# Two more gate blocks ahead of the first projection products in the merge of a hybrid attention and recurrence layer

## The reference, cut to what matters

```python
h = rms_norm(x, norm_g) * (1 + scale) + shift
qa, ka, va, za, qb, fb, ib, zb = split(h @ w_in)
ya = window_attention(qa, ka, va, sinks) * silu(za)        # width 512
o, s_new = hgrn2_chunked(qb, log_f(fb), k_in(fb), ib, s0)   # width 512
yb = rms_norm(o, o_norm_g) * silu(zb)
g_a, g_b = split(sigmoid(h @ w_merge + b_merge))            # 1024 each
y = g_a * (ya @ w_proj_a) + g_b * (yb @ w_proj_b)
out = x + gate * (y @ w_out)
```

## Time and profile before

| | |
|---|---|
| three runs, median | 1559.14 us (1557.93 to 1559.82) |
| span of the profiled execution | 1555.9 us |
| PE busy | 1527.1 us (98%) |
| DVE, ACT, POOL busy | 787.0, 540.7, 826.0 us |
| mean granted TensorE clock | 0.996 |

### The profile page before, as it was taken

How to read it: one execution, slowest core, us unless ns; L and a number is a source line. 1 busy time by engine, 2 the same in 40 slices (tenths; PEclk the granted TensorE clock), 3 DMA queues, 4 the chain that set the end, 5 groups by cost and what they waited for, 6 DMA issues and landing times.

```text
span 1555.9 us, 31655 instructions
## 1 busy us (share of the span) xinstructions
PE 1527.1 (98%) x13048; PEld 1243.0 (80%) x13048; DVE 787.0 (51%) x1900; ACT 540.7 (35%) x1119; POOL 826.0 (53%) x1074
## 2 busy tenths in 40 slices
PE   5999999999999999999999999999999999999998
PEld 2777788877888788888779878888888978888886
DVE  4767464234558866232544774622453775623132
ACT  4334324334322532434331452243432353143330
POOL 0525434557863643365773472437786363437671
PEclk9999999999999999999999999999999999999999
DMA  9612211334453321233343231223544231222351
GB/s 339 243 55 83 83 57 55 111 133 158 168 197 108 110 70 57 82 109 108 137 164 135 92 120 43 83 66 114 208 154 149 75 110 56 78 72 91 102 167 60
DMA packets 62790, 178.94 MB, mean 115 GB/s; under 512 B 7086, under 2 KB 18695, under 8 KB 61864
## 3 DMA queue, kind: packets, MB, share of 16 engines
q1 hardware_dynamic: 62648, 176.93, 33.4%
HBM read 162.84 MB, written 11.96 MB: 112 GB/s over the span
## 4 chain that ended last, share of the span: by engine, by line
PE 95%; DVE 3%; DMA 1%; SPq 1%; issue 1%; ACT 0%; DVEq 0%
PE ps_D L758 56%; PE ps_D L755 25%; PE ps_XCD L820 2%; PE ps_XB L896 1%; PE ps_XB L949 1%; PE ps_XA L954 1%; PE ps_XA L921 1%; PE ps_XA L932 1%; PE ps_XB L948 1%; PE ps_XA L896 1%; DMA th_t<-in_w_ada 1%; SPq L507 1%; PE ps_XB L932 0%; PE ps_XCD L831 0%; PE ps_XCD L939 0%
## 5 line engine op out<-in xcount | busy, mean ns | idle before, releaser
L1702 POOL TENSOR_TENSOR w_lo_t<-w_raw,w_hi_t 128x256 fp32r<-128x256 f32 x920 | 681.0, 775 | 599.7 <-ACT w_hi_t L980 599.4
L758 PE MATMUL ps_D<-h_hi_t,w_hi_t 128*128 128x512 f32 x1024 | 411.2, 402 | 0.0
L758 PE MATMUL ps_D<-h_hi_t,w_lo_t 128*128 128x512 f32 x1024 | 399.6, 390 | 0.0
L758 PE MATMUL ps_D<-h_lo_t,w_hi_t 128*128 128x512 f32 x1024 | 399.5, 390 | 0.0
L980 ACT ACTIVATE w_hi_t<-w_raw 128x1024 fp32r<-128x1024 f32 x232 | 240.0, 1051 | 124.6 <-PE ps_D L755 61.6
L758 PEld LDWEIGHTS ps_D<-h_hi_t,w_hi_t 128*128 128x128 f32 x1024 | 192.3, 188 | 46.3 <-issue 8.9
L758 PEld LDWEIGHTS ps_D<-h_hi_t,w_lo_t 128*128 128x128 f32 x1024 | 192.2, 188 | 41.8
L758 PEld LDWEIGHTS ps_D<-h_lo_t,w_hi_t 128*128 128x128 f32 x1024 | 192.6, 188 | 36.5
L755 PE MATMUL ps_D<-w_hi_t,h_hi_t 128*128 128x384 f32 (+1 forms) x384 | 141.6, 369 | 1.0 <-DVE yf_t L1342 1.0
L755 PE MATMUL ps_D<-w_lo_t,h_hi_t 128*128 128x384 f32 (+1 forms) x384 | 136.6, 356 | 0.0
L755 PE MATMUL ps_D<-w_hi_t,h_lo_t 128*128 128x384 f32 (+1 forms) x384 | 136.3, 355 | 0.0
(11 more groups left out here) (386 smaller groups left out, 2332.9 us busy)
## 6 DMA issues: line engine op xcount, KB each, us to landing
w_raw<-in_w_blocks SPq DMA_DIRECT2D x232, 512.0 KB, 3.4
xr<-in_x_prompt SPq DMA_DIRECT2D x16, 512.0 KB, 5.0
x_or_AT<-in_x_prompt SPq DMA_DIRECT2D x14, 512.0 KB, 4.8
out_dram<-xr SPq DMA_DIRECT2D x12, 512.0 KB, 2.8
x_or_AT<-in_x_turned SPq DMA_DIRECT2D x3, 1024.0 KB, 5.6
p_or_hf<-in_x_turned SPq DMA_DIRECT2D x3, 1024.0 KB, 6.2
out_dram<-xr SPq DMA_DIRECT2D x8, 256.0 KB, 2.0
ibtok<-vtok SPq DMA_DIRECT2D x8, 192.0 KB, 3.5
```

The source lines that it names most:

```text
L758: ins = mm(bank[:, :], w[:, s0, k0 + k, :], a[:, k, :], start=go, stop=end)
L1702: ins = g_.tensor_tensor(w_lo[:, c, k:k + 2], w_raw[:, n % NRAW, k:k + 2], f32(w_hi[:, c, k:k + 2]), ALU.subtract)
```

## The change

The order of the units from 36 on becomes

| units | before | after |
|---|---|---|
| 36, 37 | pa0 pb0 | ga4 gb4 |
| 38 to 41 | pa1 pb1 pa2 pb2 | pa0 pb0 pa1 pb1 |
| 42, 43 | ga4 gb4 | pa2 pb2 |
| 44, 45 | pa3 pb3 | ga5 gb5 |
| 46, 47 | ga5 gb5 | pa3 pb3 |
| 48, 49 | pa4 pb4 | ga6 gb6 |
| 50, 51 | ga6 gb6 | pa4 pb4 |
| 52 to 59 | pa5 pb5 ga7 gb7 pa6 pb6 pa7 pb7 | the same |

The weight blocks follow that order. `ga4` and `gb4` get two new places, 8 and 9, in `ff`, and ACT waits for `st 3` before it writes them. `ga5`, `ga6` and `ga7` (with their `gb`) move to places 0, 2 and 0. The tasks `xst 2` and `xst 3` move from 40.1 and 41.1 to 42.1 and 43.1. SP's event `x01` moves from 43 to 44, its event `ckv 0` from 40 to 41, and the first group of the sample attention from 43 to 44.

```diff
-    out = [(c, j) for j in range(4) for c in ("ga", "gb")]
+    out = [(c, j) for j in range(5) for c in ("ga", "gb")]
     for j in range(8):
-        out += [("pa", j), ("pb", j)] + ([("ga", j + 2), ("gb", j + 2)] if 1 < j < 6 else [])
+        out += [("pa", j), ("pb", j)] + [(c, {2: 5, 3: 6, 5: 7}[j]) for c in ("ga", "gb") if j in (2, 3, 5)]
...
-            put(it, (40, 41, 46, 47)[_n], 1, "xst", _t)
+            put(it, (42, 43, 46, 47)[_n], 1, "xst", _t)
...
-            _u = (43, 52)[_r]
+            _u = (44, 52)[_r]
...
-TH.update({(c, j): (4, 6, 0, 2, 0, 2, 0, 2)[j] + (c == "gb") for j in range(8) for c in ("ga", "gb")})
+TH.update({(c, j): (4, 6, 0, 2, 8, 0, 2, 0)[j] + (c == "gb") for j in range(8) for c in ("ga", "gb")})
...
             n = TH[(kind, j)]
+            if n >= 8:
+                return ff[:, n - 8, :]
             return th[:, n, :] if n < 4 else (R2, R3)[n // 2 - 2][:, TB * (n % 2):TB * (n % 2) + TB]
...
-                    later.setdefault(b0 + 43, []).append(("x01", it, 0))
+                    later.setdefault(b0 + 44, []).append(("x01", it, 0))
...
-            later.setdefault(40, []).append(("ckv", 0, 0))
+            later.setdefault(41, []).append(("ckv", 0, 0))
...
                     if (kind, j) == ("ga", 0):
                         s.freed(it, "PV", 3)
+                    if (kind, j) == ("ga", 4):
+                        s.freed(it, "st", 3)
```

## The result

The changed kernel takes 1561.09 us (median of 12 runs, 1559.36 to 1562.31) against 1557.45 us of the kernel before (12 runs, 1556.02 to 1559.82; its median was 1559.14 in the three runs known ahead). The ratio is 1.0021, with a 95% interval of 1.0012 to 1.0029: slower by 3.3 us. The forecast was slower by 5.0 us, and 1564 us as a time.

A forecast was written before the change was run, and what follows sets the result against it. PE's stream was taken to bound the kernel. The terms -0.2 + 1.7 + 1.5 + 2.0 = +5.0 us on the span of 1555.9 gave 1560.9, with 3.2 us around it 1564.1, forecast as 1564; range 1558.5 to 1571.5.

The forecast's parts named there:

- What bounds the kernel, and what the order can win: PE's stream bounds the kernel; PE doesn't wait for `yb_lo` at pb0, so more units in between win nothing.
- The loss through `rstd`: DVE's chain now stands between the fetches of pa4 and pb4; PE waits 1.7, 1.5 and 2.0 us in iterations 0 to 2.
- The two paces of the chain: DVE's 17 `rstd` operations take 0.20 us each with POOL idle, 0.70 with POOL working: 3.4 to 11.9 us.
- the column sum ahead of `sT 1`: Iteration 0: DVE's column sum, which empties bank XC, stands behind the chain, so PE waits 1.7 us at `sT 1`.
- The covered wait for bank D1: Iteration 2: pb5 needs D1, freed by pb4's fetch at 1126.3; `bc` keeps PE busy to 1126.4, so no added wait.
- the sum's negative side: Iteration 1 on PE: pa4 and pa5 become neighbours, two `bu` become one pair; -0.2 us, ends 0 and -0.6.
- the term for the time around the span: 3.2 us added around the forecast span of 1560.9 us to give the time of 1564.1 us.
- (a): Rival, chance 0.20: POOL idle when `rstd` starts, the chain takes 3.4 us and is hidden; not slower, 1559 us.
- (b): Rival, chance 0.12: the chain stays 7.8, 6.3 and 10.3 us long; waits together 12.3 us, time 1571 us.
- (c): Rival, chance 0.07: the cache rows come late in iteration 0, +2.4 us, 1566.5 us.
- (d): Rival, chance 0.06: each of three PE waits is followed by 3 us at half clock, 1.5 us more each, 1568.5 us.
- (e): Rival, chance 0.05: faster, PE's 1.5 and 0.7 us waits vanish; with the `bu` pair 2.4 us, 1557 us.

The follow-up runs named there:

- experiment 2: Changed kernel with PE's `bc` one unit later (53.1 instead of 52.1), `rstd` left in place; 1562.83 us, ratio 1.0032 to the kernel before.
- experiment 6: Kernel before with the sample attention's two groups a unit later (44 and 53 instead of 43 and 52); 1557.11 us, ratio 0.9996.
- experiment 4: Changed kernel with the split of block `pa6` on ACT and POOL moved from unit 50 to 52 in iterations 0 to 2; 1562.12 us.
- experiment 3: Changed kernel with 12 more operations in the `rstd` chain, 29 instead of 17, in iterations 0 to 2; 1574.43 us.

## Why the prediction was right and wrong

**What bounds the kernel, and what the order can win.** Right. PE's stream sets the end, and pa0 and pb0 are fetched without a wait in both orders. Iteration 3, which has the new order and nothing else, is unchanged to 0.01 us.

**The loss through `rstd`.** Right in mechanism and place, and near in size. The prediction had 1.7, 1.5 and 2.0 us for the three iterations, 5.2 together. Taking the chain out of the sandwich gave back 1.65, 1.51 and 1.84, together 5.0. The two paces of the chain, POOL's schedule that sets their mix and the column sum ahead of `sT 1` came as worked out. In iteration 2 the chain was to end at 1125.6 and `bc` to be due at 1123.65, with the second kernel's start as before; the profile has 1124.7 and 1123.27, an earlier start of the iteration and a slightly shorter wait. The covered wait for bank D1 is there as well: experiment 2 uncovered it.

**The step that failed** is the sum's negative side, and beside it the term for the time around the span. The prediction said that "the matmuls, splits and weight blocks are the same in number" and that one side effect saves PE work, "I take -0.2". The pair came (L814 of 128x128 falls from 64 to 32 instructions in iteration 1) and was worth -0.41. Larger is what was left out: the sample tasks of iteration 0 move too, and their own queue for bank XC was not gone through in the old order. Against the kernel before, the changed order with `rstd` at 49.0 is 1.30 us shorter in iteration 0, and experiment 6 finds 1.06 in the old order by moving the sample tasks alone. That these are the same 1.06 is an inference from the two waits on bank XC, which are absent in both kernels. The remaining 0.24 is not settled by a run; `bu` and `sO` standing together within pa4 is only a candidate. Two of these waits could be read before: the 0.4 us at L839 and the 0.2 us at L831 in PE's waits of iteration 0. I had looked only for long ones. The sum with the measured terms is 5.0 - 0.41 - 1.30 = +3.3 us, the measured 3.3 of the ratio (a further 0.16 us in units 28 to 59 of iteration 1 is not accounted for). The negative side was thus put at -0.2 where -1.7 was measured.

The time of 1564 (1564.1 before it was rounded) was 3.0 us too long, and only 1.4 of that is the sum (5.0 forecast, 3.6 by the medians). Another 1.0 is the 3.2 us taken to lie around the span. In every execution whose span is listed beside its time, the time is 2.1 to 2.2 us the longer. The 3.2 came from setting the median of three runs against the span of another execution. The last 0.6 is that the profiled execution, at 1555.9, was longer than the median of twelve runs less this remainder, 1555.3.

**The rivals.** (a), the hidden chain, fell: it was 6.0 us in iteration 2, 5.7 in iteration 1 and 4.8 in iteration 0, nowhere under 4.4. (b), a chain as long as before, fell too, since POOL's next work does depend on it. (c), late cache rows, didn't occur: with the chain gone, `sT 1` doesn't wait, though its loads hadn't moved. (d), clock lost behind a wait, didn't occur at waits of 1.3 to 1.6 us, nor at 1.9 and 2.2 (experiment 2, where the granted clock is 1.00 around both). It did at 3.7, 3.8, 3.9 and 4.0. The Trainium skill ("TensorE: Matmul & The Clock Gate", section "HAM oscillation") ties the fall to waits of TensorE on data; the traces agree, with 0.50 granted after each of these four. (e) was half true: the order did have gains, but of other waits than those two, and the loss outweighed them.

## What to carry to other kernels

When units of a hand-written order are swapped, go through the queue of every engine, not only the one that sets the end. Ask for each side task whether it now stands between two operations that release something, as a latency-bound chain of 17 tiny operations did between the fetches of two banks. Put such a chain where its engine has nothing to release; that one place was worth 5.0 us here and turned a version 0.21% slower into one 0.14% faster (ratio 0.9986), the fastest median of all that were run. The stretches put its lead over the kernel before at about 1.5 us, apart from the issue wait. Read the short waits as well: moving the sample tasks so that two of 0.2 and 0.4 us on a shared bank fell away won 1.06 us. And take what lies around the span from the time and the span of one and the same execution.

## What the runs showed of the hardware

- An operation of 4 columns on DVE follows each 0.20 us with POOL idle and each 0.70 us with POOL at work, whether it is a tensor-tensor or a tensor-scalar operation. In experiment 4 one tensor-scalar operation of 512 columns was held for 5.90 us, through eight POOL instructions in a row, and a tensor-tensor operation took 1.28 us in one execution of the changed kernel and 6.87 in another. The Trainium skill ("SBUF — State Buffer", section "Who interferes with whom") has the loser block until the other's instruction has finished. The 0.70 pace agrees with that. The 5.90 us don't: that operation wasn't let in between POOL's instructions, while the small ones were. What decides between the two was not tried.
- With the four waits of 3.7 to 4.0 us that the runs have after 242 us (three in experiment 3, one in experiment 4) the granted clock fell to 0.50; after waits of up to 2.2 us it stayed at 1.00. It fell 0.9 and 0.7 us before the wait's end in two of them and stayed down for 6.8 us; in the other two it fell at the wait's end and 1.4 us behind it and stayed down for 3.4 us. On top of the wait the first two cost 2.8 and 2.7 us, the others 1.6 and 1.5.
- The wait put down to issue at the start of the output projection of iteration 1 took 0.7, 0.8, 1.0, 1.5 and 1.6 us in different executions, and both 0.8 and 1.5 in one and the same kernel.
